# A one-core encoder block with a routed expert stage: the last batch's weights in halves, the residual through the identity, and a reordered closing norm

## The reference

```python
h = _layer_norm(ALPHA * x + mix, ln1_g, ln1_b)
ffn = _moe(h, ...)      # 64 experts, top 8 of 4 of 8 groups, plus a shared expert
return _layer_norm(ALPHA * h + ffn, ln2_g, ln2_b)

def body(y, blk):       # one expert on its tokens
    hid = silu(xb @ w_gate[e]) * (xb @ w_up[e])
    out = (hid @ w_down[e]) * gate[:, None]
    return y.at[tok].add(out), None
```

## Time and profile before

| | us |
|---|---|
| runs (three): median, lowest, highest | 831.35, 831.22, 833.11 |
| span of the profiled execution, first to last instruction | 829.7 |
| TensorE busy | 758.2 (91%) |
| VectorE busy | 271.1 (33%) |
| ScalarE busy | 157.3 (19%) |
| moved by DMA | 246.70 MB |

### The profile page before, as it was taken

How to read it: one execution, slowest core, us unless ns; L and a number is a source line. 1 busy time by engine, 2 the same in 40 slices (tenths; PEclk the granted TensorE clock), 3 DMA queues, 4 the chain that set the end, 5 groups by cost and what they waited for, 6 DMA issues and landing times.

```text
span 829.7 us, 11397 instructions
## 1 busy us (share of the span) xinstructions
PE 758.2 (91%) x4703; PEld 445.3 (54%) x4704; DVE 271.1 (33%) x683; ACT 157.3 (19%) x337; POOL 10.8 (1%) x24
## 2 busy tenths in 40 slices
PE   5999999898999998999999999698798896999971
PEld 4888887666886445544544444244253343444430
DVE  0703963455465118422221222121121111122216
ACT  0110032326453004211211112011021111111111
POOL 1000000000000001000000000000000000000000
PEclk9999999999999999999999999899799899999997
DMA  9933443321231349799999999999999999999931
GB/s 303 384 141 150 152 152 102 104 100 58 95 102 65 152 160 419 276 372 389 390 387 429 425 421 429 425 424 426 422 426 427 424 427 420 427 424 424 427 163 51
DMA packets 26002, 246.70 MB, mean 297 GB/s; under 512 B 3568, under 2 KB 3840, under 8 KB 4704
## 3 DMA queue, kind: packets, MB, share of 16 engines
q1 hardware_dynamic: 24768, 241.31, 71.3%
q0 software_dynamic: 1184, 4.67, 1.7%
HBM read 245.06 MB, written 1.05 MB: 297 GB/s over the span
## 4 chain that ended last, share of the span: by engine, by line
PE 73%; DMA 20%; DVE 5%; ACT 1%; issue 1%; SPq 0%; DVEq 0%; ACTq 0%
PE bank L567 20%; DMA arena<-in_we_dram 19%; PE bank L894 19%; PE bank L936 6%; PE bank L715 6%; PE bank L847 5%; PE bank L856 4%; PE bank L690 3%; DMA arena<-in_xT_dram 1%; PE bank L764 1%; PE bank L669 1%; PE bank L585 1%; PE bank L912 1%; PE bank L805 1%; PE bank L589 1%
## 5 line engine op out<-in xcount | busy, mean ns | idle before, releaser
L894 PE MATMUL bank<-arena 128*64 128x512 f32 (+1 forms) x1024 | 193.8, 644 | 32.7 <-DMA arena<-in_we_dram 32.7
L567 PE MATMUL bank<-arena 128*128 128x256 f32 x768 | 172.8, 381 | 0.0
L567 PEld LDWEIGHTS bank<-arena 128*128 128x128 f32 x768 | 145.0, 190 | 19.8
L894 PEld LDWEIGHTS bank<-arena 128*64 128x64 f32 (+1 forms) x1024 | 53.9, 132 | 130.9 <-issue 128.4
L936 PE MATMUL bank<-arena 128*64 128x512 f32 (+1 forms) x512 | 91.3, 597 | 0.7 <-issue 0.7
L847 PEld LDWEIGHTS bank<-onehotb,h_part 128*128 128x128 bf16 x1248 | 69.8, 98 | 20.3 <-issue 20.3
L1481 DVE COPY arena<-bank 64x1 f32<-64x1 f32 (+1 forms) x64 | 9.9, 155 | 209.2 <-PE bank L912 208.7
L847 PE MATMUL bank<-onehotb,h_part 128*128 128x128 bf16 x1248 | 74.2, 219 | 0.8 <-ACT arena L1088 0.8
L1500 DVE TENSOR_TENSOR y_lo<-bank,y_hi 128x512 fp32r<-128x512 f32 x50 | 34.6, 692 | 100.9 <-ACT y_hi L1115 75.1
L715 PE MATMUL bank<-arena 128*128 128x512 f32 x128 | 55.7, 593 | 0.3 <-DVE arena L1192 0.3
L936 PEld LDWEIGHTS bank<-arena 128*64 128x64 f32 (+1 forms) x512 | 25.9, 125 | 52.8 <-issue 46.3
(11 more groups left out here) (241 smaller groups left out, 512.5 us busy)
## 6 DMA issues: line engine op xcount, KB each, us to landing
arena<-in_we_dram SPq DMA_DIRECT2D x64, 2048.0 KB, 20.5
arena<-in_we_dram SPq DMA_DIRECT2D x64, 1024.0 KB, 26.1
arena<-in_wc_dram SPq DMA_DIRECT2D x12, 1024.0 KB, 16.1
arena<-in_wn_dram SPq DMA_DIRECT2D x12, 1024.0 KB, 4.8
arena<-in_wo_dram SPq DMA_DIRECT2D x8, 1024.0 KB, 4.8
arena<-in_ln_dram POOLq DMA_DIRECT2D x2, 1024.0 KB, 8.9
arena<-in_ws_dram SPq DMA_DIRECT2D x1, 2048.0 KB, 8.0
arena<-in_wgi_dram SPq DMA_DIRECT2D x2, 512.0 KB, 7.1
```

Of the source, the lines that this page charges most:

```text
L567: mm = nc.tensor.matmul(bank[n % 2][:, j * S:(j + 1) * S], wk, xk, start=(k == 0), stop=(k == KD - 1))
L894: mm = nc.tensor.matmul(bank[0][rows[q], :], hc[v][:, k, rows[q]], slot[places[q]][:, k * 512:(k + 1) * 512], start=(k == 0), stop=(k == K ...
```

## The change

1. **Halves.** The last batch of the loop is loaded by `load_last` instead of two `load_pair`: the gate and up weights of all four experts for `k` 0 to 3, then those for `k` 4 to 7, then columns 0 to 511 of the four down weights, then 512 to 1023. That is 16 loads for 8, with the same bytes. `free_gu` of slots 2 and 3 is now waited for before `free_down` of slots 0 and 1. A half of `GU` is 8 KB in a row of a partition (before: 16 KB); a half of `DOWN` is two pieces of 2 KB (before: 8 KB in a row). In this batch (`closes`) TensorE waits for the second half of `GU` before `k == 4` and for the second half of `DOWN` before `half == 1`.
2. **Residual.** `ALPHA * h` is no longer added on VectorE. After batch 9, twelve bf16 matmuls with the identity (`residual`) add the three parts of `h` to the accumulators. To balance it the gates and the shared hidden are scaled by `1 / ALPHA`, and `EPS` by `1 / ALPHA ** 2`.
3. **Closing.** After the last batch TensorE scatters by half, not by `t`, the last matmul of each accumulator closes it, and the zero tile is gone. VectorE takes `bn_stats` from the four accumulators, then one `bn_aggr` for each `t`, and one variance, one square root and one `rsqrt` for both; `centre` subtracts the mean and applies the gain straight from PSUM.

```diff
+GU_HALF = (slice(0, KD * 256), slice(KD * 256, KD * 512))
...
+def closes(b, turn):
+    return turn is not None and b == TURN_B - 1
...
+def load_last(b, turn):
+    loads = batch_loads(b, turn)
+    jobs = []
+    for q in range(LAST):
+        sp.reg_load(last_number[q], eid[0:1, bass.ds(column(b, turn) + q, 1)])
+        jobs.append(sp.snap(last_number[q], min_val=0, max_val=E - 1))
+    down = [slot[q][:, DOWN].rearrange("p (f n) -> p f n", f=2) for q in range(LAST)]
+    def source(q, part):
+        return a["we"][bass.ds(jobs[q], 1)].rearrange("o p n -> (o p) n")[:, part]
+    for q in range(LAST):
+        if q % 2 == 0:
+            sp.wait_ge(free_gu[q // 2], uses(loads[q], turn))
+        sp.dma_start(slot[q][:, GU_HALF[0]], source(q, GU_HALF[0])).then_inc(last_gu[q], 16)
+    for q in range(LAST):
+        sp.dma_start(slot[q][:, GU_HALF[1]], source(q, GU_HALF[1])).then_inc(slot_gu[q], 16)
+    for q in range(LAST):
+        if q % 2 == 0:
+            sp.wait_ge(free_down[q // 2], uses(loads[q], turn))
+        src = source(q, DOWN).rearrange("p (f n) -> p f n", f=2)
+        sp.dma_start(down[q][:, :, 0:512], src[:, :, 0:512]).then_inc(last_down[q], 16)
+    for q in range(LAST):
+        src = source(q, DOWN).rearrange("p (f n) -> p f n", f=2)
+        sp.dma_start(down[q][:, :, 512:D], src[:, :, 512:D]).then_inc(slot_down[q], 16)
...
-    for b in range(TURN_B):
+    for b in range(TURN_B - 1):
...
+    load_last(TURN_B - 1, j)
...
-    sp.wait_ge(out_ready, t + 1)
+    sp.wait_ge(out_ready[t], 1)
...
+def residual():
+    for t in range(T):
+        for half in range(2):
+            for i in range(3):
+                nc.tensor.matmul(bank[4 + 2 * t + half][:, :], identb[:],
+                                 h_part[i][:, t, half * 512:(half + 1) * 512],
+                                 start=False, stop=False, skip_group_check=True)
     for q in range(w):
-        pe.wait_ge(slot_gu[places[q]], (uses(loads[q], turn) + 1) * 16)
+        if closes(b, turn):
+            pe.wait_ge(last_gu[q], (turn + 1) * 16)
+        else:
+            pe.wait_ge(slot_gu[places[q]], (uses(loads[q], turn) + 1) * 16)
     for k in range(KD):
+        if k == KD // 2 and closes(b, turn):
+            for q in range(w):
+                pe.wait_ge(slot_gu[places[q]], (uses(loads[q], turn) + 1) * 16)
         for q in range(w):
...
     for q in range(w):
-        pe.wait_ge(slot_down[places[q]], (uses(loads[q], turn) + 1) * 16)
+        if closes(b, turn):
+            pe.wait_ge(last_down[q], (turn + 1) * 16)
+        else:
+            pe.wait_ge(slot_down[places[q]], (uses(loads[q], turn) + 1) * 16)
     for half in range(2):
+        if half == 1 and closes(b, turn):
+            for q in range(w):
+                pe.wait_ge(slot_down[places[q]], (uses(loads[q], turn) + 1) * 16)
...
     if b == SHARED_AFTER:
...
+    if b == RESIDUAL_AFTER:
+        residual()
...
-pe.wait_ge(ylo_ready, n_turns * (2 * TURN_B) + 2 * FIRST_B)
-for t in range(T):
-    scatter(t, 0)
-    for half in range(2):
-        mm = nc.tensor.matmul(bank[4 + 2 * t + half][:, :], zb[:], zb[:, 0:1].to_broadcast([P, 512]),
-                              start=False, stop=True, skip_group_check=True)
-    mm.then_inc(moe_ready, 1)
+for half in range(2):
+    pe.wait_ge(ylo_ready, n_turns * (2 * TURN_B) + (2 * FIRST_B - 1 + half))
+    c = slice(half * 512, (half + 1) * 512)
+    for t in range(T):
+        nc.tensor.matmul(bank[4 + 2 * t + half][:, :], onehotT[0][:, t, :], y_hi[:, c],
+                         start=False, stop=False, skip_group_check=True)
+        nc.tensor.matmul(bank[4 + 2 * t + half][:, :], onehotT[0][:, t, :], y_lo[:, c],
+                         start=False, stop=True, skip_group_check=True).then_inc(moe_ready, 1)
...
-    nc.scalar.activation(hh[:, t, :], bank[7 * t][:, FE:2 * FE], ACT.Copy).then_inc(sh_silu, 1)
+    nc.scalar.activation(hh[:, t, :], bank[7 * t][:, FE:2 * FE], ACT.Copy, scale=1.0 / ALPHA
+                         ).then_inc(sh_silu, 1)
-for t in range(T):
-    act.wait_ge(var_ready, 5 + t)
-    nc.scalar.activation(vv[:, 1, t:t + 1], vv[:, 0, t:t + 1], ACT.Sqrt).then_inc(sqrt_done, 1)
+roots(slice(0, T), 5)
...
 def gates(t):
...
-    link(V.tensor_scalar(gate[:, t, :], cand, need[:, 1:2], ROUTED_SCALE, ALU.mult, ALU.mult))
+    link(V.tensor_scalar(gate[:, t, :], cand, need[:, 1:2], ROUTED_SCALE / ALPHA, ALU.mult,
+                         ALU.mult))
...
+for half in range(2):
+    for t in range(T):
+        dve.wait_ge(moe_ready, 2 * half + t + 1)
+        ins = V.bn_stats(stat[:, 2 * t + half, :], bank[4 + 2 * t + half][:, :])
+link(ins)
+for t in range(T):
+    ins = V.bn_aggr(mv[:, t, :], stat[:, 2 * t:2 * t + 2, :].rearrange("p a b -> p (a b)"))
+link(ins)
+V.tensor_scalar(vv[:, 0, 0:T], mv[:, 0:T, 1], EPS / ALPHA ** 2, None, ALU.add).then_inc(var_ready, 1)
+dve.wait_ge(var_ready, 5)
+def centre(t):
+    for half in range(2):
+        c = slice(half * 512, (half + 1) * 512)
+        ins = V.scalar_tensor_tensor(out=ytmp[:, t, c], in0=bank[4 + 2 * t + half][:, :],
+                                     scalar=mv[:, t, 0:1], in1=ln2[:, 0, c], op0=ALU.subtract,
+                                     op1=ALU.mult)
+    return ins
...
-layer_norm(h, ytmp, ln2, 5, out_ready, 4, moe_ready, (1, 2))
+link(centre(0))
+rsqrt(slice(0, T), 5)
+for t in range(T):
+    if t == 1:
+        link(centre(1))
+    V.scalar_tensor_tensor(out=ytmp[:, t, :], in0=ytmp[:, t, :], scalar=vv[:, 3, t:t + 1],
+                           in1=ln2[:, 1, :], op0=ALU.mult, op1=ALU.add).then_inc(out_ready[t], 1)
```

More of the change, by code:

```diff
@@ L101 @@
 SHARED_AFTER = 5
+RESIDUAL_AFTER = 9
+LAST = 4
 NPK = 24
@@ L275, in build @@
         free_down = [sem(f"free_down{i}") for i in range(RING // 2)]
+        last_gu = [sem(f"last_gu{q}") for q in range(LAST)]
+        last_down = [sem(f"last_down{q}") for q in range(LAST)]
         sh_down = sem("sh_down")
@@ L344, in build @@
         moe_ready = sem("moe_ready")
-        out_ready = sem("out_ready")
+        out_ready = [sem(f"out_ready{t}") for t in range(T)]
         s_dve = sem("s_dve")
@@ L396, in column @@
             return turn * RJ + (TURN[b % TURN_B][1] + b // TURN_B * RJ)
+        def closes(b, turn):
+            return turn is not None and b == TURN_B - 1
+        assert [n % RING for n in range(TURN_LOADS - LAST, TURN_LOADS)] == list(range(LAST))
         def width(b, turn):
@@ L432, in _ @@
             number = [sp.alloc_register(f"number{q}") for q in range(2)]
+            last_number = [sp.alloc_register(f"last_number{q}") for q in range(LAST)]
             def load(place, e, part, full):
```

## The result

| us | before | changed |
|---|---|---|
| median of five runs each, taken together | 833.11 | 819.08 |
| lowest, highest | 831.22, 834.32 | 817.42, 823.08 |
| span of the profiled execution | 829.7 | 820.6 |

The ratio is 0.9843 with a 95% interval of 0.9821 to 0.9864; the forecast of 819.4 us against 831.35 is 0.9856. The kernel is 1.6% faster. Two later comparisons of the same changed kernel gave 0.9859 (0.9834 to 0.9884) and 0.9846 (0.9821 to 0.9871), at 820.52 and 819.38 us.

A forecast was written before the change was run, and what follows sets the result against it. The prediction took weight loads at about 425 GB/s, and everything exposed behind the last weights, as the bound. Gains of 6.5 and 5.5 us took 831.35 to 819.4 us; range 817.3 to 823.8.

The forecast's parts named there:

- The pause and the clock: Last batch: TensorE's 5.05 us load wait and about 1.4 us of slow clock go; 6.5 us gained.
- the landing table: Last batch's loads at 2.45 us per MB: gate/up halves at 779.7 and 789.5, down halves at 794.4 and 799.3.
- The slack before `half == 1`: Last batch: second down halves land at 799.3, TensorE asks at 801.5; 2.2 us to spare.
- The moved wait and the 2 KB pieces: Last batch's loads: reordered slot waits on SP leave the queue full and short down pieces keep full rate; zero cost.
- rival A: Last batch: short down pieces run slower, halves land late, `half == 1` waits; mostly 820 to 823 us, chance 0.12.
- the two bounds: Rates for the 2 KB down pieces: 420 GB/s costs nothing more; 223 GB/s leaves no gain from the halves.
- the 0.33 us for each issue: Last batch: SP issues sixteen loads for eight at some 0.33 us each, with more than 20 us of loads queued.
- an estimate of 5% at 2 KB: Down loads, last batch: packet cost of 67 for 64 cycles, 0.5 us of 9.8, hidden by 2.2 us to spare.
- The residual: Twelve matmuls after batch 9, up to 3.7 us, hidden by the 6.30 us load pause before batch 10; zero.
- The tail: From the last `y_lo` to the span's end: VectorE works without a gap, 13.1 us for 18.6; 5.5 gained.
- its lower end (12.6): Closing on VectorE: instructions without a wait between them may overlap by some tenths, 12.6 us instead of 13.1.
- the forecast 817.7: Whole kernel's profiled span: 829.7 less 6.5 and 5.5 us gives 817.7.

The follow-up runs named there:

- the whole loads: Changed kernel with eight whole loads for sixteen halves, gate and up before down: 818.92 us, beside 820.52 for the changed kernel.
- the closing alone: Changed kernel with the last loads whole and in pairs as before, residual and closing as changed: 826.40 us, before 831.88.

## Why the prediction was right

**The pause and the clock (6.5 us).** Right in mechanism and size: alone the part gave 6.65, and TensorE takes 13.87 us for the last batch (13.80). What it named as cause was too wide: the new order does it, and the cut into halves adds nothing while the gather stands ahead of the batch. For the gate weights the landing table was good to some tenths of a microsecond: it has them down at 789.5 when TensorE is free, and the whole loads show a gap of 0.42 us exactly there. For the last `DOWN` halves it was 1.1 us too early, as follows.

**The slack before `half == 1` (2.2 us).** Right in sign, and its size in the first profile is luck. Count from the turn's first gate matmul (704.66 before): by the forecast TensorE asks for the last halves at 801.5, so at 96.8, and the last landing is at 94.6. The changed kernel asks at 803.25 + 1.8 = 805.1, so at 97.9, and the last load (issued at 791.1, 11.9 us to landing) is down at 95.8: 2.1 us to spare, since both times came about 1.1 us later. In its third profile it asks at 96.6 (798.80 + 1.8 - 704.02) and the load (issued at 787.8, 12.1 us to landing) is down at 95.9: 0.7 us to spare, 1.5 less than forecast. The landing is late in both, by 1.2 us, and that is mostly the price of the short rows (with 4 KB rows in as many loads it is 95.0), which the forecast had at zero. The time of asking moved with the turn's first batch, whose forty matmuls took 7.37 us at slow clock in the first profile and 6.13 in the third. That batch ends on TensorE's time and the loads do not care for it. So the slack depends on where the clock comes back there, which I had not taken in, and only a long slow clock made up for the late landing in the first profile. This is also why leaving out the gather pays about half of what I expected.

**The moved wait and the 2 KB pieces (zero).** On the end of the kernel both cost nothing, as forecast. The moved wait costs the loads nothing either: the whole loads have it too, and their last landing is where it was before (94.7 us for 94.6). The queue doesn't run dry: the slices stay at 417 to 428 GB/s. The pieces do cost the loads something, 0.5 to 0.9 us against 4 KB and some 1.1 against whole loads, hidden by the slack. So rival A had a true mechanism at a size that the slack covers. Of the two bounds the 420 GB/s was near the truth and the 223 GB/s far from it. What was wrong is the 0.33 us for each issue: the halves of `DOWN` were issued far more slowly (last section), the last one only 11.9 us ahead of its landing, where the forecast had more than 20. The windows of the changed kernel show the rate (busy and count by engine, PEclk, DMA share, GB/s):

```profile
785.00:790.00 5.00, 5.00 (x24) 1.90 (x22) 1.28 (x3) 0.60 (x1) 0.00 (x0) 1.00 1.01 411
790.00:795.00 5.00, 5.00 (x70) 3.36 (x72) 0.69 (x1) 1.79 (x3) 0.00 (x0) 1.00 1.04 388
795.00:797.00 2.00, 2.00 (x24) 0.52 (x16) 0.00 (x0) 0.00 (x0) 0.00 (x0) 1.00 1.05 384
```

With the short pieces in flight the engines are as full as before, and 384 to 388 GB/s come out for 425, a loss of 9%; on the 9.8 us of the down weights that is 0.9 us. From the fixed cost for each packet in the Trainium skill, DMA: Bandwidth & Descriptors, section "Why small descriptors are slow (HBM only)", the prediction had an estimate of 5% at 2 KB; the direction holds, the measured loss is larger. The same page of the Trainium skill, section "Measured (HBM->SBUF, 128 partitions, SWDGE, issued from GpSimd)", asks for 1 MiB a load or more to have 75% of the peak. It measured loads from GpSimd; here loads of 512 KB with 4 KB rows in a full queue from SP lost far less than a quarter (last landing at 95.0 us against 94.7, over 9.8 us of loads).

**The residual (zero).** Right: 2.76 us of matmuls in a pause that shrank from 6.10 to 3.65 us, and 1.8 us when it stands at the end.

**The tail (5.5 us).** Right, 0.7 too small: 12.4 us and not 13.1. Four statistics that don't wait for each other took 2.49 us and not 2.9, two `bn_aggr` 0.29 and not 0.5; that is the overlap that the prediction named as its lower end (12.6). Leaving the loop costs TensorE nothing to be seen: the last down matmul ends at 806.8, and the first scatter matmul starts at 806.75. Of the parts of these 6.2 us only the early half 0 was taken back by itself (0.9). An estimate of the rest from the rows of before and after: the first statistic starts 0.1 us before the last `y_lo` ends, where VectorE stood for 1.8 us before, 1.9 in all with that 0.9; the four additions are gone, 2.9 at 0.72 each; and the small steps of `t` 1 are gone, 1.4. No run shows these two apart.

**The absolute place.** The profiled span is 2.9 us above the forecast 817.7. Of this 2.5 lie before the turn (707.18 for 704.66) and 1.0 in the slow clock of the turn's first batch (7.37 for 6.36); the tail gives 0.7 back. The other four of that comparison had spans of 815.6 to 818.0, and all sixteen executions of this kernel 815.6 to 820.8. That the measured gain of the first comparison is 14.0 us and not 12.0 comes mostly from the other side: there the kernel before had 833.11, and the forecast stood on 831.35, which is 1.8 of the 2.0. The start of the turn moves by up to 4 us between executions (703.2 to 707.2 over the kernels here), and most of it is there at batch 10 already (524.7 to 528.5); what moves it was not examined.

## What to carry to other kernels

At the end of a stream of loads ask in which order the last consumer uses them and what is left to do after each landing; a change of order alone can remove the last wait, and finer pieces are worth something only if the engine would be there earlier. List landings and the times at which they are asked for side by side, to a tenth of a microsecond: here they told a removed wait from a moved one before the run, but the last landing came 1.2 us later than listed, over half of the 2.2 us to spare. A closing chain on one engine shrinks by taking small steps once for all tiles and by folding additions into an engine that waits anyway.

## What the hardware showed that I had not expected

- SP took far longer to issue loads with short rows. In the kernels before and with whole loads each issue takes 333 ns, and so does each half of `GU` with its 8 KB rows. In the changed kernel the `DOWN` halves of 2 KB pieces take up to 4.5 us each (first line: ns of an issue, minimum, median, maximum; then issue to landing); with 4 KB rows the median is 1.99 us. That a limit on the rows outstanding is behind it is my guess; no run shows it. It cost no time to be seen here, since the queue stayed full and SP has nothing else to do in that stretch.

```profile
L496 SPq DMA_DIRECT2D arena<-in_we_dram x4: 392/3971/4542, 770.9 to 779.8; - x4
DMA to landing us min/median/max: 18.0/21.9/23.7
```

- Once TensorE and not the loads sets the end, its clock in the turn's first batch shows in the time: the forty gate matmuls there took 5.79 to 7.45 us from profile to profile, and nothing behind them absorbs it. With the old loads the pause at the last batch did, for the most part: 6.36 us there and a pause of 5.05 before, 7.37 and 4.41 with the closing alone.
- A gap of 0.42 us left the granted clock at 1.00 in the forty matmuls behind it. Behind the one of 2.97 us (whole loads without the gather) it was 0.79 in the microsecond from 789 and 0.50, half clock, in the next, with eight matmuls done in each:

```profile
789.00:790.00 1.00, 0.79 (x8) 0.46 (x12) 0.00 (x0) 0.00 (x0) 0.00 (x0) 0.79 0.98 410
790.00:791.00 1.00, 1.00 (x8) 0.27 (x4) 0.00 (x0) 0.00 (x0) 0.00 (x0) 0.50 1.00 418
```
